# One block for merge, routing and experts; GpSimd subtractions during routing; first gathers without index copies

## What is computed

```python
yp = yp + merge_branches(oa, ob, ga, gb, w_branch_a, w_branch_b, w_out)
yp = yp + moe_ffn(yp, norm2_g, w_rg, b_rg, w_re, b_re, w_gate, w_up, w_down)

def hier_moe(h, ...):                       # h: rms_norm of the rows
    gl = h @ w_rg + b_rg                    # 4 groups, the best one is taken
    gidx = argmax(gl); gw = softmax(gl)[gidx]
    el = (h @ w_re + b_re).reshape(n, 4, 4)[gidx]
    top_l, top_i = top_k(el, 2)             # two experts of that group's four
    combine = one_hot(gidx * 4 + top_i) * softmax(top_l) * gw
    hid = silu(h @ w_gate[e]) * (h @ w_up[e]) * combine   # 16 experts, 256 wide
    return hid @ w_down[e]
```

## Time and profile before

| | us |
|---|---|
| median of 3 runs (1071.09 to 1075.38) | 1071.72 |
| profiled execution | 1073.2 |
| its span, from the first to the last instruction | 1071.5 |
| TensorE busy (matmul) | 946.7 (88%) |
| VectorE busy | 465.6 (43%) |
| ScalarE busy | 353.8 (33%) |
| GpSimd busy | 230.1 (21%) |

### The profile page before, as it was taken

How to read it: one execution, slowest core, us unless ns; L and a number is a source line. 1 busy time by engine, 2 the same in 40 slices (tenths; PEclk the granted TensorE clock), 3 DMA queues, 4 the chain that set the end, 5 groups by cost and what they waited for, 6 DMA issues and landing times. The chain is left out here.

```text
span 1071.5 us, 16297 instructions
## 1 busy us (share of the span) xinstructions
PE 946.7 (88%) x5399; PEld 853.6 (80%) x5400; DVE 465.6 (43%) x859; ACT 353.8 (33%) x577; POOL 230.1 (21%) x252
## 2 busy tenths in 40 slices
PE   3999999879798999999999979999149999879993
PEld 3888887668698999999999979998137887657782
DVE  3566655533221222222122154433754657766520
ACT  5545443310032211111111131221324557666431
POOL 2545411014422000000000010000022454444431
PEclk9999999679999999999999989999569999899996
DMA  7100100220020101111010036742147989999653
GB/s 197 40 21 21 44 20 25 60 81 1 7 85 30 59 30 59 39 49 59 29 59 29 20 123 231 265 160 83 43 176 261 274 258 324 352 350 336 148 121 66
DMA packets 66128, 124.19 MB, mean 116 GB/s; under 512 B 6384, under 2 KB 41392, under 8 KB 66064
## 3 DMA queue, kind: packets, MB, share of 16 engines
q1 hardware_dynamic: 56064, 95.24, 26.0%
q0 software_dynamic: 7488, 27.27, 10.3%
q10 hardware_dynamic: 2528, 1.06, 0.4%
HBM read 101.57 MB, written 23.00 MB: 116 GB/s over the span
## 5 line engine op out<-in xcount | busy, mean ns | idle before, releaser
L1237 ACT ACTIVATE gate<-psum 128x352 f32<-128x352 f32 x48 | 22.3, 464 | 226.9 <-PE psum L65 226.9
L63 PE MATMUL psum<-w_hi,hT_hi 128*128 128x512 f32 (+3 forms) x216 | 81.9, 379 | 12.8 <-DVE w_lo L745 8.2
L1933 DVE TENSOR_TENSOR hT_lo<-room,hT_hi (+1 forms) x32 | 72.0, 2290 | 29.7 <-ACT hT_hi L1778 29.7
L63 PE MATMUL psum<-hT_hi,x_xT_hi 128*128 x192 | 79.1, 412 | 2.5 <-ACT x_xT_hi L1789 1.1
L65 PE MATMUL psum<-w_hi,hT_lo 128*128 128x512 f32 (+3 forms) x216 | 78.5, 364 | 0.0
L64 PE MATMUL psum<-w_lo,hT_hi 128*128 128x512 f32 (+3 forms) x216 | 78.5, 364 | 0.0
L63 PE MATMUL psum<-hT_hi,w_hi 128*128 128x352 f32 x240 | 77.4, 323 | 0.0
L64 PE MATMUL psum<-hT_lo,w_hi 128*128 128x352 f32 x240 | 76.9, 321 | 0.0
L65 PE MATMUL psum<-hT_hi,w_lo 128*128 128x352 f32 x240 | 76.9, 320 | 0.0
L65 PE MATMUL psum<-hT_hi,x_xT_lo 128*128 x192 | 76.6, 399 | 0.0
L64 PE MATMUL psum<-hT_lo,x_xT_hi 128*128 x192 | 76.6, 399 | 0.0
(11 more groups left out here) (337 smaller groups left out, 2409.1 us busy)
## 6 DMA issues: line engine op xcount, KB each, us to landing
room<-in_w_gu SPq DMA_DIRECT2D x16, 2048.0 KB, 11.2
dn_raw<-in_w_dn SPq DMA_DIRECT2D x16, 1024.0 KB, 6.3
g_w_raw<-in_w_ab SPq DMA_DIRECT2D x15, 768.0 KB, 4.4
xT_chunk<-in_xT SPq DMA_DIRECT2D x8, 528.0 KB, 3.9
x_in<-in_x SPq DMA_DIRECT2D x8, 512.0 KB, 3.5
out_y<-y SPq DMA_DIRECT2D x8, 512.0 KB, 3.8
hn_rows<-squares SPq DMA_DIRECT2D x8, 512.0 KB, 3.2
o_w_raw<-in_w_out_t SPq DMA_DIRECT2D x7, 512.0 KB, 8.0
```

The source lines that it names most:

```text
L63: eng.matmul(out, lh, rh, start=first and k == 0, stop=False)
L1237: act.activation(gate[:, (ab + c) % 2, :], bank(psum, pair(ab, c))[:, 0:TC], ACT.Sigmoid).then_inc(gated.sem, 1)
L1933: dve.tensor_tensor(gu_lo[:, buf, ks], gu_raw[:, buf, ks], gu_hi[:, buf, ks].bitcast(F32), ALU.subtract).then_inc(gu_lo_made.sem, 1)
```

## The change

Both phases become one block. What follows is its core; names that only move are left out.

- There is no meeting of engines between merge and routing. Semaphores do what it did: VectorE waits for the last `summed`, and, ahead of the one-hot tables (which now lie in rows of `y`), for the stores.
- VectorE's gain of the last chunk moves behind the two instructions that sum up the squares.
- ScalarE makes `up_high(0, 0)` ahead of the last `keep_y`, then the others and both `down_high` during routing.
- GpSimd makes all four low halves of gate and up, from its power on; VectorE keeps both `down_low`, now ahead of the first tokens' low half.
- Both `hot` tables are made first; two of the six `in_step` products go to GpSimd, and TensorE's second part waits for them.
- SyncE issues the loads of experts 2 and 3 as soon as the halves of 0 and 1 are there; from expert 4 on the order is as before.
- The first four gathers read `gather_at` directly.
- The tests of a round are nested in the first one.

```diff
+            for f in (at_made, at_copied, add_turn, gu_lo_made):
+                f.begin(pool)
+            pool.sem_inc(at_made.sem, RING)
+            pool.wait_ge(meaned, 1)
+            pool.tensor_tensor(r2[:, :], yss[:, :], consts["minus_half"][:, :], ALU.pow).then_inc(rooted, 1)
+            for n in range(2):
+                for half in range(2):
+                    ks = slice(half * KH, (half + 1) * KH)
+                    gu_hi_made.wait(pool, 2 * n + half)
+                    pool.tensor_tensor(gu_lo[:, n, ks], gu_raw[:, n, ks], gu_hi[:, n, ks].bitcast(F32),
+                                       ALU.subtract).then_inc(gu_lo_made.sem, 1)
+            pool.wait_ge(hot_made, 1)
+            for v, value in ((1, wts[:, 1, :]), (2, r2[:, :])):
+                pool.tensor_tensor(in_step[:, 1, :, v, :], hot[:, 1, :, :], value.unsqueeze(2).broadcast_to([P, NT, PLANNED]),
+                                   ALU.mult).then_inc(second_in_step, 1)
...
             pool.wait_ge(gather_made, 1)
-            for s in range(RING):
-                gather(s, s)
+            for r in range(RING):
+                pool.indirect_dma_start(xg[:, r, :], None, io["hn"], bass.IndirectOffsetOnAxis(gather_at[:, r:r + 1], 0)).then_inc(gathered[r], DMA)
...
+            act.wait_ge(gu_landed, 2)
+            act.wait_ge(made, 3 * KD)
+            up_high(0, 0)
+            keep_y(KD - 1)
+            up_high(0, 1)
+            up_high(1, 0)
...
             act.wait_ge(g_shifted, 1)
             act.activation(g_exp[:, :, :], g_exp[:, :, :], ACT.Exp).then_inc(g_exped, 1)
+            up_high(1, 1)
+            act.wait_ge(evicted, 3 * KD)
+            down_high(0)
             act.wait_ge(e_shifted, 1)
             act.activation(ratio[:, :], ratio[:, :], ACT.Exp).then_inc(e_exped, 1)
+            down_high(1)
             tokens_high(0, 0)
...
+            dve.wait_ge(summed, KD)
+            did(dve.tensor_reduce(yss[:, :], square_sums[:, :, :], AX_X, ALU.add))
             dve.tensor_scalar(yss[:, :], yss[:, :], 1.0 / D, EPS, ALU.mult, ALU.add).then_inc(meaned, 1)
+            gain(KD - 1)
             dve.wait_ge(rooted, 1)
...
+            dve.wait_ge(stored, DMA * (KD + 2))
+            dve.wait_ge(hn_stored, DMA * 2 * KD)
+            for n in (1, 0):
+                ins = dve.tensor_tensor(hot[:, n, :, :], consts["steps"][:, :].unsqueeze(1).broadcast_to([P, NT, PLANNED]),
+                                        over_last(slot_hi[:, n, :], PLANNED), ALU.is_equal)
+                ins.then_inc(hot_made, 1)
+            dve.wait_ge(hot_made, 2)
...
-            up_low(0, 0)
             dve.wait_ge(found_made, 1)
...
-            up_low(0, 1)
-            tokens_low(0, 0)
-            for half in range(2):
-                up_low(1, half)
             for n in range(2):
                 down_low(n)
+            tokens_low(0, 0)
+            gu_lo_made.wait(dve, 3)
...
             with eng.Fori(1, MOST_STEPS // RING) as i:
+                with eng.If(i * RING + 1 <= used):
+                    step(i * RING, 0)
+                    for r in range(1, RING):
+                        with eng.If(i * RING + (r + 1) <= used):
+                            step(i * RING + r, r)
...
+            for i in (2, 3):
+                load_up(i)
+            landed(2)
+            for i in (2, 3):
+                load_down(i)
+            down_landed(2)
+            for i in range(3, NE):
+                landed(i)
+                if i + 1 < NE:
+                    load_up(i + 1)
+                down_landed(i)
+                if i + 1 < NE:
+                    load_down(i + 1)
```

More of the change, by code:

```diff
@@ L1 @@
+import math
 from contextlib import ExitStack
@@ new lines, in merge_moe_phase @@
+        yss, r2, g_top, pr_top, ratio, g_sum = (brief([NT]) for _ in range(6))
+        logits = brief([NT, NR])
+        g_exp, g_pick = brief([NT, NG]), brief([NT, NG])
+        eq, e_sel = brief([NT, EPG]), brief([NT, EPG])
+        sel4 = brief([NT, NG, EPG])
+        e_top, wts = brief([2, NT]), brief([2, NT])
+        e_pick = brief([2, NT, EPG])
+        chosen = brief([2, NT, NG, EPG])
+        before = brief([NE, NT + 1])
+        over, place = brief([NE, NT]), brief([NE, NT])
+        steps_of, step_end = brief([NE]), brief([NE])
@@ L1363, in split, with over_steps, splits_of, experts_of @@
             return keep["first_o"] if d == 0 else (w_hi[:, d % 2], w_lo[:, d % 2])
+        def over_steps(eng, step, last):
+            used = eng.value_load(step_plan[0:1, 0, PLANNED:PLANNED + 1], min_val=NE, max_val=MOST_STEPS)
+            for s in range(RING):
+                step(s, s)
+            with eng.Fori(1, MOST_STEPS // RING) as i:
+                with eng.If(i * RING + 1 <= used):
[3 more added lines that the diff above has]
+                            step(i * RING + r, r)
+            last(used)
+        def splits_of(eng, s):
+            return eng.value_load(step_plan[0:1, 0, bass.ds(s, 1)], min_val=0, max_val=4 * NE - 1)
+        def experts_of(eng, s):
+            return eng.value_load(step_plan[0:1, 1, bass.ds(s, 1)], min_val=0, max_val=NE * NE - 1)
+        def first(s):
+            return isinstance(s, int) and s == 0
+        def times(s, r):
+            return (s - r) * (DMA // RING) + DMA
         @block.sync
@@ new lines, in scatter @@
+            def scatter(s, j):
+                out_made.wait(pool, s)
+                pool.tensor_copy(put_at[:, j:j + 1], scatter_at[:, bass.ds(s, 1)]).then_inc(at_copied.sem, 1)
+                at_copied.wait(pool, s)
+                if not first(s):
+                    pool.wait_ge(added, s * DMA)
+                pool.sem_inc(add_turn.sem, 1)
+                pool.indirect_dma_start(io["y"], bass.IndirectOffsetOnAxis(put_at[:, j:j + 1], 0), out[:, j, :], None,
+                                        compute_op=ALU.add).then_inc(added, DMA)
@@ L1440, in _ @@
+            pool.wait_ge(stored, DMA * (KD + 2))
+            pool.wait_ge(hn_stored, DMA * 2 * KD)
+            pool.wait_ge(gather_made, 1)
+            for r in range(RING):
+                pool.indirect_dma_start(xg[:, r, :], None, io["hn"], bass.IndirectOffsetOnAxis(gather_at[:, r:r + 1], 0)).then_inc(gathered[r], DMA)
+            pool.wait_ge(slots_made, 1)
+            over_steps(pool, step, last)
         @block.scalar
@@ new lines, in hidden_high, with evict, step @@
+            def hidden_high(s):
+                hidT_made.wait(act, s)
+                down_made.wait(act, s - 1)
+                act.activation(hidT_hi[:, :, :].rearrange("p k c -> p (k c)"), bank(psum, 4)[:, 0:DE], ACT.Copy).then_inc(hidT_hi_made.sem, 1)
+            def evict(s, row):
+                down_made.wait(act, s)
+                add_turn.wait(act, s - 1)
+                act.activation(row, psum[:, 5:7, :].rearrange("p a c -> p (a c)"), ACT.Copy).then_inc(out_made.sem, 1)
+            def step(s, r):
+                j = r % 2
+                if not first(s):
+                    hidden_high(s - 1)
+                plan = splits_of(act, s)
+                up_made.wait(act, s)
+                hid_made.wait(act, s - 1)
+                act.activation(silu, bank(psum, 2 + j)[:, 0:DE], ACT.Silu, scale=slot_wr[:, 1, bass.ds(s, 1)]).then_inc(silu_made.sem, 1)
+                tokens_high(s + 1, 1 - j)
+                with act.If(plan % 2 > 0):
+                    n = plan // 4 + 2
+                    act.wait_ge(gu_landed, n + 1)
+                    for half in range(2):
+                        up_high(n, half)
+                if not first(s):
+                    evict(s - 1, out[:, 1 - j, :])
+                    with act.If(plan // 2 % 2 > 0):
+                        down_high(plan // 4 + 1)
@@ L1467, in _ @@
+            over_steps(act, step, last)
         @block.tensor
@@ L1513, in _ @@
             back(KD - 1)
[L1515 to L1573, removed]
@@ new lines, in gain @@
+            def gain(d):
+                dve.wait_ge(y_copied, d + 1)
+                dve.wait_ge(summed, d + 1)
+                dve.tensor_tensor(squares[:, :, :], y[:, :, chunk(d)], g2_rows[:, chunk(d)].unsqueeze(1).broadcast_to([P, NT, P]),
+                                  ALU.mult).then_inc(gained, 1)
+            for k in range(KD):
+                dve.wait_ge(h2_hi, k + 1)
+                dve.tensor_tensor(hT[1][:, k, :], h2[:, k, :], hT[0][:, k, :].bitcast(F32), ALU.subtract).then_inc(h2_lo, 1)
@@ new lines, in _ @@
+            dve.wait_ge(const_in, DMA * 4)
+            dve.tensor_tensor(w_r[:, :, :], w_r[:, :, :], g2[:, :].unsqueeze(2).broadcast_to([P, KD, NR]), ALU.mult).then_inc(w_r_made, 1)
+            dve.wait_ge(made, 3)
+            dve.memset(squares[:, PT, :], 0.0).then_inc(zeroed, 1)
+            dve.wait_ge(zeroed, 3)
+            for d in range(KD):
+                if d + 1 < KD:
+                    weights(d + 1)
+                evict(d, 0)
+                if d > 0:
+                    rest(d - 1)
```

(4 more changed lines are left out.)

419 lines of the change are left out of this document (171 added, 248 removed).

## The result

| | before, us | after, us |
|---|---|---|
| median | 1071.72 (1071.04 to 1075.38, 5 runs) | 1079.92 (1078.76 to 1081.47, 5 runs) |
| profiled execution | 1073.2 | 1078.76 |
| its span | 1071.5 | 1077.0 |
| mean granted clock in it | 0.943 | 0.941 |

The ratio is 1.0066, 95% interval 1.0052 to 1.0081: the changed kernel is slower by about 0.7% (7.1 us, 5.6 to 8.7). The medians lie 8.2 us apart, the two profiled executions only 5.6: that of before is slower than its median, that of after is the fastest of its five runs.

The account below looks back on a forecast made before the run. Routing (VectorE's serial chain), weight loads and TensorE were taken to bound the kernel in turn. +7.9 - 0.65 - 2.6 = +4.6 us on the profiled execution, 1076.3 on the median (1.5 lower); likeliest case 1072 to 1082, stated range 1062 to 1083.

Parts of the forecast that it names:

- Part 1: Boundary between merge and routing: without it the sum over chunks starts 4.8 us earlier, the logits 3.5 earlier.
- Part 2: Logits to hot tables: GpSimd's four half subtractions shut out VectorE's two-input instructions, +17.1 us; hot tables +13.5.
- Rival A: Routing: long GpSimd instructions don't lock VectorE out, or GpSimd's work overlaps; -14.8 us, 1056.9; chance 0.13.
- Rival B: Logits to fourth half: lock price per half above 4.62 us makes it over 0.5% slower; slower overall given 0.39.
- Part 3: Hot tables to gather indices: 11.4 us instead of 12.12, -0.7; indices at +12.8.
- Part 4: First gathers: TensorE starts 6.7 us after the indices instead of 11.61, -4.9; transposes at +7.9.
- the toss: First gather's issue against VectorE's down-projection half: either may go first; issue ends at +2.0 or +4.4 us.
- The copies gone: Index copies ahead of the first gathers: removal saves only 0.2 to 0.5 us; the 0.96 is the gather's issue.
- Part 5: Step 0: hidden part runs sooner, -0.35 us, and a shorter idle before its half-clock stretch, -0.3.
- Shift passing through: Expert steps, load-bound ones too: routing's gain or loss moves them all alike and passes through whole.
- Part 6: Nested Ifs at the end: tests save 1.3 to 1.4 us, TensorE idle 3.0, kept clock half-booked -1.2; together -2.6.
- Sum: Whole kernel against the profiled 1073.2 us: +7.9 - 0.65 - 2.6 = +4.6.

Follow-up runs that it names:

- e2: Changed kernel with nobody making the four gate/up low halves, GpSimd only signalling: 1063.5 us, ratio 0.9930 against the kernel before.
- e1: Changed kernel with VectorE making the four gate/up low halves in their old places instead of GpSimd: 1065.77 us, ratio 0.9946 against the kernel before.
- e8: Changed kernel with GpSimd copying the four raw halves instead of subtracting: 1068.59 us, ratio 0.9966 against the kernel before.
- e6: Changed kernel with the down loads of experts 2 and 3 held until the first gather has landed: 1077.71 us, ratio 1.0055.
- e3: Changed kernel with only expert 0's two halves on GpSimd, expert 1's on VectorE behind the first tokens' low part: 1068.67 us, ratio 0.9973.
- e7: Changed kernel with VectorE making all four gate/up halves, meant to follow the first gather's issue by a bare GpSimd increment: 1062.33 us, ratio 0.9905.
- e10: e9 with index copies restored in front of the first four gathers, with a plain wait: 1061.17 us, ratio 0.9892 against the kernel before.
- e4: Kernel before with the nested Ifs alone: 1069.84 us, ratio 0.9980.
- e5: Changed kernel with both down-projection low halves moved behind the first tokens' low parts: 1076.8 us, ratio 1.0039 against the kernel before.
- e9: e7 with the signal on a one-element GpSimd memset in place of the bare increment: 1060.89 us, ratio 0.9894 against the kernel before.

## Why the prediction was right, and where it wasn't

The predicted 1076.3 lay 3.6 below the measured 1079.92; faster 0.17, same 0.44, slower 0.39, and slower came, which had not been the likeliest. On the profiled executions, on which the sum was made, +4.6 was predicted and +5.6 came.

**Part 1**: right. The sum starts at 751.00 (predicted 750.55; the merge itself ends 0.47 later in this execution), the power beside the gain takes 2.87 instead of 1.83, the logits come at 754.42: -3.3 for -3.5. No run tests the boundary alone; this is read from the trace.

**Part 2**: right, and it decides. Four times 4.42 less 0.5 gave 17.1; the stretches measure 16.6, and e2 takes 16.6 out of the chain and 14.9 (profiled) to 16.4 (medians) out of the time. The half takes 4.55 on the mean for 4.61. The fit from 352 and 512 elements carried to 2048. Hot tables +13.3 for +13.5. Rival A is out by e1 and e2. Rival B did not come about as told: its cause was a half above 4.62, and they are below; the outcome on its side has other causes (below). One reading in this part failed without a price: ScalarE's high halves did bind. The exponential came behind VectorE's third stretched instruction, not its second, so GpSimd stood idle for 2.20 ahead of the fourth half; VectorE's small instructions ran at 0.2 in that time, and the chain still paid four halves.

By the Trainium skill (SBUF — State Buffer, "SBUF: two separate sides") GpSimd and a two-input VectorE instruction exclude each other for the whole instruction: the trace agrees with 4.15 to 4.63 for an instruction of 36 or 180 elements. That section of the Trainium skill has this against any GpSimd operation that reads SBUF, and e8 agrees: a GpSimd copy of 1.9 does the same. The Trainium skill (GPSIMD Engine Reference, 3.1) has 4.497 for a `tensor_tensor` add of 2048 elements; the four subtractions took 4.50 to 4.60, nearer to it than the fit's 4.61 on the whole.

**Part 3**: -1.4 instead of -0.7, indices +11.9 for +12.8. The first pair was ready 0.4 sooner (4.58 for 5.0), and TensorE took 6.00.

**Part 4**: here a step failed. 6.7 was predicted from indices to TensorE and 9.74 came: 1.0 of it is the toss and 2.0 the loads. The toss was lost (issue 3.21; the end at +4.4 as priced for that case), and the sentence "The 1 MB loads, released by dn_lo, land behind the first gather" was wrong: the first load is released by the first `down_low` alone, 1.0 before the gather's issue ends, and e6 prices the sharing at 2.0. The toss was no toss either: in the kernel after and in e1, e2, e3, e6, e7 and e8 VectorE's subtraction led each time by 0.16 to 0.18, and the issue took 3.2. It should have been a certain +4.4, and both loads drawn against it. "The copies gone" are worth what was booked: the issue starts 1.16 behind the indices in the kernel after and 1.52 before, 0.36 for 0.2 to 0.5. Its reason, that the 0.96 behind a copy is the gather's own issue, holds only in part: with a plain wait (e10) that idle is 0.65 and the whole copy costs 0.07. Why the old wait takes 0.3 longer stays open.

**Part 5**: the -0.65 did not come. Silu of step 0 comes +10.4 and that of step 1 +10.0, against TensorE's start at +10.0; `hid` follows TensorE's start by 11.83 instead of 12.02, which is all that shows. The -0.3 for a shorter idle had the wrong sign: the idle was 9.85 instead of 14.32, yet the stretch with matmuls 0.43 apart was longer, 5.25 instead of 4.41.

**Shift passing through**: nearly. 1.0 of 10.0 was absorbed between 921 and 1057 us, where idle times for the loads sum to 10.8 instead of 12.7; the prediction named this as a way to be wrong and gave it nothing.

**Part 6**: idle 3.08 for 3.0, right (e4: 3.06). The clock held in this execution, worth 2.4 at the last output copy for the half-booked 1.2, but 0.7 of it went into a wait that was not foreseen: the last scatter is now late for the one before it, whose DMA lands 1.0 after the last index copy. In this execution a still shorter tail would gain nothing more by TensorE. In eleven profiled kernels with an idle of 3.06 to 3.13 the clock held throughout in three (the kernel after, e5, e8) and fell for all or part of the last 12 matmuls in eight.

**Sum** (profiled): +10.0 (for 7.9), nothing from step 0 (for -0.65), -1.0 in the load-bound stretch (for 0), -1.3 tests (-1.4), -2.4 + 0.7 clock and scatter (-1.2), -0.5 behind the last issue (0) = +5.5 (for +4.6). That the sum came so near is in part luck: part 4's miss of +3.0 was covered by 0.9 from parts 1 to 3, 0.35 in the loop and 0.9 in the tail, which have nothing to do with it.

**From profile to median**: -1.5 was taken over from before; it is +1.2 in the kernel after. That 2.7 is most of the remaining 3.6. The profiled 5.6 alone lies on the prediction's own line between "same" and "slower" (5.4); by the ratio it is 7.1, so a part of the 2.7 may be how five runs of each kernel fell. The runs of the kernel after spread by 2.7 us, those of e5 by 3.8, and in both the time goes with the granted clock (after: 1078.76 at 0.941, the others 1079.62 to 1081.47 at 0.937 to 0.938; e5: 1074.3 to 1074.5 at 0.942 to 0.943, 1076.4 to 1078.2 at 0.936 to 0.940). A clock lost in the tail would make 1.7 of it by the rows above; where the other runs lose theirs stays open, as only one run of each has a trace.

## What to carry to other kernels

Moving work to an idle GpSimd is not free while VectorE runs a serial chain of small two-input instructions: count nearly GpSimd's whole duration as if it stood in that chain, once per instruction (4.16 of 4.55 and 1.54 of 1.95 here), however small VectorE's instructions are. Such work belongs where VectorE's chain is waiting for something else, here behind the first gather's issue, and on the faster engine (2.3 us a half for 4.55); GpSimd in that same place was not tried. An expected tie between two engines for a shared resource should be read from the order in which both are dispatched, not booked at half. One profiled execution lay up to 2.3 us beside its kernel's median (e5 below it, e4 2.1 above it), which matters when the whole effect is 5.

## What the runs showed of the hardware

- A semaphore increment that stands alone behind an indirect DMA on GpSimd doesn't wait for the DMA's issue: VectorE, released by it, began at 779.01, the issue at 779.17 (e7). On a memset it came behind the issue's end (780.76; VectorE at 780.92, e9; e10 alike).
- GpSimd's issue of an indirect DMA is held up by VectorE's two-input subtraction too (3.21 to 3.23 when a half starts just ahead of it, 0.94 to 1.23 without). e6, with the loads held back and the subtraction kept, still has 3.22.
- From the end of the first gather's issue to TensorE it is 3.38 to 3.47 with no weight load beside it (e6, e5), 5.37 with the 1 MB loads (the kernel after) and 7.07 with a 2 MB load (e1).
- A GpSimd copy with conversion, one input of 2048 elements, 1.89 to 2.01 us, excludes VectorE's two-input instructions as the subtraction does.
- The issue starts 1.15 us behind the start of the instruction that writes the indices; with an index copy and a plain wait in between it is 1.22 (e10), with the wait of the kernel before 1.52.
